# The even layer of a two-block network: four projection stages on tiles, rewritten as one stage of tile pairs with seven block products

## The reference, cut to what matters

```python
def even_layer(x, norm_g, w_in, pool_w, pool_scale, ws, bs, w_out):
    h = rmsnorm_2(x, norm_g)
    z = h @ w_in
    a, g_a, u, v, g_b = jnp.split(
        z, [A_WIDTH, 2 * A_WIDTH, 2 * A_WIDTH + B_WIDTH, 2 * A_WIDTH + 2 * B_WIDTH], axis=-1)
    y_a = multiscale_pool(a, pool_w, pool_scale) * jax.nn.silu(g_a)
    y_b = chunk_spatial_gate(u, v, ws, bs) * jax.nn.silu(g_b)
    return x + jnp.concatenate([y_a, y_b], axis=-1) @ w_out
```

## Time and profile before

| | us |
|---|---|
| median of 3 runs (3453.51 to 3455.23) | 3454.36 |
| the profiled execution, its own time | 3456.07 |
| its span in the profile | 3454.1 |
| PE busy | 3201.6 (93%) |
| DVE busy | 1726.1 (50%) |
| POOL busy | 1461.1 (42%) |
| ACT busy | 1195.2 (35%) |

### The profile page before, as it was taken

One profiled execution on the slowest core, in us unless ns is written; L12 is line 12 of the kernel. 1 busy time (PEld: TensorE's weight loads), 2 busy tenths in 40 slices (PEclk: granted clock), 3 DMA queues, 4 the chain that ended last, 5 costly groups with the idle time before them and its releaser, 6 DMA issues. The chain is left out here.

```text
span 3454.1 us, 43574 instructions
## 1 busy us (share of the span) xinstructions
PE 3201.6 (93%) x16242; PEld 2624.9 (76%) x16242; DVE 1726.1 (50%) x2541; ACT 1195.2 (35%) x2015; POOL 1461.1 (42%) x916
## 2 busy tenths in 40 slices
PE   4978997969599879999999799999999999999998
PEld 3767885857488757777887588888888888888877
DVE  4566224753799653311112565565555556555712
ACT  4256122732477621101101244443443444322311
POOL 2320331132422223333333265565565556688732
PEclk7989998989799999999999899999999999999999
DMA  8130113054699941141112211111111111222331
GB/s 288 43 86 30 41 40 102 2 178 140 243 397 396 335 135 45 31 146 52 43 43 97 72 49 46 47 56 44 55 45 48 47 46 56 66 75 74 112 104 68
DMA packets 310445, 347.46 MB, mean 101 GB/s; under 512 B 27894, under 2 KB 279722, under 8 KB 303986
## 3 DMA queue, kind: packets, MB, share of 16 engines
q1 hardware_dynamic: 299820, 308.21, 26.7%
q0 software_dynamic: 4608, 16.78, 1.9%
q10 hardware_dynamic: 5830, 19.98, 1.5%
HBM read 290.14 MB, written 51.38 MB: 99 GB/s over the span
## 5 line engine op out<-in xcount | busy, mean ns | idle before, releaser
L275 POOL TENSOR_TENSOR w_hi<-w_raw,zero_col 128x1024 fp32r<-128x1024 f32 x73 | 139.0, 1904 | 714.7 <-PE mls_z L310 205.3
L3087 POOL TENSOR_TENSOR odd_quarter_lo<-odd_w_sums,odd_quarter_hi 128x512 fp32r<-128x512 f32 x224 | 299.7, 1340 | 278.0 <-ACT odd_quarter_hi L3082 276.4
L3122 PE MATMUL first_z<-odd_t_hi,odd_quarter_hi 128*128 128x512 f32 x784 | 327.5, 418 | 18.7 <-DVE odd_t_lo L3830 18.7
L3122 PE MATMUL odd_z<-odd_t_hi,odd_quarter_hi 128*128 128x512 f32 x784 | 325.8, 416 | 0.1
L3124 PE MATMUL first_z<-odd_t_hi,odd_quarter_lo 128*128 128x512 f32 x784 | 308.4, 393 | 0.0
L3123 PE MATMUL first_z<-odd_t_lo,odd_quarter_hi 128*128 128x512 f32 x784 | 307.1, 392 | 0.0
L3124 PE MATMUL odd_z<-odd_t_hi,odd_quarter_lo 128*128 128x512 f32 x784 | 307.0, 392 | 0.0
L3123 PE MATMUL odd_z<-odd_t_lo,odd_quarter_hi 128*128 128x512 f32 x784 | 305.6, 390 | 0.0
L3087 POOL TENSOR_TENSOR odd_quarter_lo<-odd_raw,odd_quarter_hi 128x512 fp32r<-128x512 f32 x168 | 231.3, 1377 | 168.1 <-ACT odd_quarter_hi L3082 163.7
L3082 ACT CAST odd_quarter_hi<-odd_w_sums 128x512 fp32r<-128x512 f32 x224 | 139.6, 623 | 365.0 <-PE odd_z L3124 179.1
L3138 DVE SCALAR_TENSOR_TENSOR dil_set<-first_z,dil_set 128x512 f32<-128x512 f32 x196 | 170.6, 883 | 143.5 <-PE first_z L3124 138.4
(11 more groups left out here) (598 smaller groups left out, 7680.1 us busy)
## 6 DMA issues: line engine op xcount, KB each, us to landing
odd_raw<-in_odd_w_in SPq DMA_DIRECT2D x224, 256.0 KB, 3.1
raw_gate<-in_w_gate SPq DMA_DIRECT2D x16, 2048.0 KB, 16.2
raw_up<-in_w_up SPq DMA_DIRECT2D x16, 2048.0 KB, 15.1
raw_down<-in_w_down SPq DMA_DIRECT2D x16, 2048.0 KB, 15.7
w_raw<-in_even_w_in SPq DMA_DIRECT2D x40, 512.0 KB, 3.7
start_w_mod<-in_w_mod SPq DMA_DIRECT2D x11, 1024.0 KB, 10.9
w_raw<-in_w_in SPq DMA_DIRECT2D x16, 512.0 KB, 3.6
scan_w_mod<-in_w_mod SPq DMA_DIRECT2D x8, 1024.0 KB, 11.3
```

Of the source, the lines that this page charges most:

```text
L275: pool.tensor_tensor(w_hi[:, u], w_raw[:, u], zero_col[:, 0:1].to_broadcast([P, KT * P]).rearrange("p (k n) -> p k n", k=KT), ALU.add).the ...
L3087: pool.tensor_tensor(self.w_lo[:, n % self.SLOTS], self.source(m, i), self.w_hi[:, n % self.SLOTS].bitcast(F32), ALU.subtract).then_inc(se ...
L3122: pe.matmul(to, self.w_hi[:, slot, kt], t_hi[:, kt], start=(kt == 0), stop=False)
```

## The change

The even layer becomes one stage, `phase_even`, with the norm at its head. Its 40 projection tiles are taken in 20 pairs by `Quarters`: 8 pairs for the pool groups (per group one pair of `a` tiles and one pair of `g_a` tiles) and 4 triples of pairs (`v`, gate, `u`) for the spatial part. The mixing products (`mix_pool`, `turn_v`, `mix_spatial`) are put between block products of a later pair. The pool's running sums on DVE are cut in six parts (`pool_part`) that stand between the joins of the group's second pair. The `y` tiles are stored to DRAM and read back, and then one output product runs over all 2048 channels (`unit`: 16 units of 48 matmuls, one tile over half of the channels each), so the residual is read and written once. The prefetch in the expert stage is gone: the first weights are loaded at the head of the new stage. `Quarters` itself is unchanged but stands ahead in the file.

```diff
-        def phase_pool(next_parts, first_z):
...
-        def phase_spatial(next_parts, first_z):
...
-        def phase_even_norm(first_z):
...
+        phase_experts()
         first_z = ctx.enter_context(nc.psum_tensor("first_z", [P, 2, HALF], F32))
...
-        phase_even_norm(first_z)
-        phase_pool([even_a_out(u) for u in range(2)], first_z)
-        phase_out("even_a_out", y_hi, y_lo, even_a_out, 1, None, [even_cols(u, slice(SPATIAL_COLS[u], SPATIAL_COLS[u] + P)) for u in range(2)],
-                  first_z=first_z, first_done=True, next_rhs=(h_hi, h_lo))
-        phase_spatial([even_b_out(u) for u in range(2)], first_z)
...
+        def phase_even(first_z):
...
+            G, POOL_PAIRS, TRIPLES = len(POOL_SIZES), 2 * len(POOL_SIZES), KT // 2
+            PAIRS = POOL_PAIRS + 3 * TRIPLES
+            B11, T2_SUM, T3_SUM, T4_SUM, T1_SUM, B21, B22 = range(7)
...
+            quarters = Quarters("even", Arena(nc, quarters_at), PAIRS)
...
+            def pair_cols(m):
+                if m < POOL_PAIRS:
+                    return [pool_col(2 * m + t) for t in range(2)]
+                j, kind = (m - POOL_PAIRS) // 3, (m - POOL_PAIRS) % 3
+                return [SPATIAL_COLS[kind] + (2 * j + t) * P for t in range(2)]
...
+            def unit(k):
+                if k < 4:
+                    return k % 2, KT * (k // 2)
+                return k // 2, KT * (k % 2)
...
+                    for g in range(GROUPS):
+                        for j in (2 * g, 2 * g + 1):
+                            sp.dma_start(rows[:, j, :], ffn_rows[j * P:(j + 1) * P, :]).then_inc(rows_loaded[g], 16)
+                    load(0)
...
+                    for g in range(GROUPS):
+                        sp.wait_ge(added, KT * (g + 1))
+                        sp.dma_start(of_tokens(x_cm_k, g), of_tokens(even_xt, g)).then_inc(x_stored, 16)
+                    sp.wait_ge(x_stored, 16 * GROUPS)
+                    sp.wait_ge(scaled_done, GROUPS)
+                    load_matrices(0)
+                    load_matrices(1)
+                    for m in range(1, PAIRS):
...
+                    sp.wait_ge(y_done, KO)
+                    sp.dma_start(odd_x[:], x_cm_k).then_inc(x_loaded, 16)
+                    for k in range(4, 2 * KT):
+                        load_unit(k)
...
+                    for m in range(PAIRS):
+                        quarters.pool(pool, m)
...
+                    spread_out(3)
+                    pe.wait_ge(masked, 1)
+                    for g in range(G):
+                        ins = pe.transpose(aux[:, 1, g * CHUNK:(g + 1) * CHUNK], ws_low[:, g, :], ident)
+                    ins.then_inc(ws_turned, 1)
+                    def multiply(m, i, between=None):
+                        if m == 0:
+                            pe.wait_ge(t_lo_done, i + 1)
+                        quarters.multiply(pe, m, i, banks, even_tokens, between)
+                    def mix_pool(g, part):
+                        d, b = part // 2, part % 2
+                        if part == 0:
+                            pe.wait_ge(w_pool_loaded[g % 2], 16 * (g // 2 + 1))
+                            pe.wait_ge(pooled_done, 2 * g + 2)
+                            pe.wait_ge(y_done, 2 * g)
+                        for k in range(2):
+                            ins = pe.matmul((acc, aux)[d][:, b, :], w_pool[:, g % 2, k, d * P:(d + 1) * P], pooled[:, k, b * HALF:(b + 1) * HALF],
+                                            start=(k == 0), stop=(k == 1))
+                        if part == 3:
+                            ins.then_inc(pool_mixed, 1)
...
+                    for g in range(G):
+                        for i in range(7):
+                            multiply(2 * g, i)
+                            if g and 2 <= i < 6:
+                                mix_pool(g - 1, i - 2)
+                        for i in range(7):
+                            multiply(2 * g + 1, i)
+                    for j in range(TRIPLES):
+                        m = POOL_PAIRS + 3 * j
+                        for i in range(7):
+                            multiply(m, i)
+                            if j == 0 and 2 <= i < 6:
+                                mix_pool(G - 1, i - 2)
+                        for i in range(7):
+                            multiply(m + 1, i)
+                            if i < 2:
+                                turn_v(j, i)
+                        for i in range(7):
+                            multiply(m + 2, i)
+                            if 1 <= i < 5:
+                                mix_spatial(j, (i - 1) // 2, (i - 1) % 2)
+                    for k in range(2 * KT):
+                        n, first = unit(k)
+                        u = k % 2
+                        pe.wait_ge(wo_split, k + 1)
+                        if k < 2:
+                            pe.wait_ge(quarters.evicted, 7 * (PAIRS - 1) + (5, 7)[k])
+                        elif n >= 2 and first == 0:
+                            pe.wait_ge(z_free, n - 1)
+                        for kt in range(KT):
+                            c = first + kt
+                            if k in (0, 2):
+                                pe.wait_ge(y_lo_done, c + 1)
+                            for w, rhs, begin, end in ((wo_hi, y_hi[c], c == 0, False), (wo_hi, y_lo[c], False, False), (wo_lo, y_hi[c], False, c == KO - 1)):
+                                for b in range(2):
+                                    ins = pe.matmul(z[n % 2][:, b, :], w[:, u, kt], rhs[:, b * HALF:(b + 1) * HALF], start=begin, stop=end)
+                        ins.then_inc(projected, 1)
...
+                    square(3)
+                    root(2)
+                    quarters.hi(act, 0)
+                    quarters.hi(act, 1)
+                    root(3)
+                    act.wait_ge(scaled_done, 2)
+                    token_hi(B11, scaled[:, K1, T1])
+                    quarters.hi(act, 2)
+                    quarters.hi(act, 3)
+                    act.wait_ge(scaled_done, GROUPS)
+                    act.wait_ge(x_stored, 16 * GROUPS)
+                    token_hi(B21, scaled[:, K2, T1])
+                    token_hi(B22, scaled[:, K2, T2])
+                    for n, i in enumerate((T1_SUM, T2_SUM, T3_SUM, T4_SUM)):
+                        act.wait_ge(t_added, n + 1)
+                        token_hi(i, even_sums[i][:])
+                    def hi(m, i):
+                        quarters.hi(act, 7 * m + i + quarters.SLOTS)
...
+                        quarters.p1(act, m, banks, targets(m))
+                        hi(m, 0)
+                        if m < POOL_PAIRS + 1 and m % 2 == 0 and m:
+                            act.wait_ge(quarters.evicted, 7 * (m - 1) + 7)
+                            act.activation(silu[:], silu[:], ACT.Silu).then_inc(pool_silu, 1)
+                        if m >= POOL_PAIRS and kind == 2:
+                            act.wait_ge(quarters.evicted, 7 * (m - 1) + 7)
+                            act.activation(g_cm[:], g_cm[:], ACT.Silu).then_inc(spat_silu, 1)
+                        hi(m, 1)
+                        hi(m, 2)
...
+                    scale(3)
+                    b11, b12, b21, b22 = scaled[:, K1, T1], scaled[:, K1, T2], scaled[:, K2, T1], scaled[:, K2, T2]
+                    token_lo(B11, b11)
+                    dve.wait_ge(scaled_done, GROUPS)
+                    token_sum(T1_SUM, b12, b11)
+                    dve.wait_ge(t_added, 1)
+                    token_sum(T2_SUM, b22, even_sums[T1_SUM][:])
+                    token_sum(T3_SUM, b22, b12)
+                    dve.wait_ge(t_added, 2)
+                    token_sum(T4_SUM, b21, even_sums[T2_SUM][:])
+                    dve.wait_ge(t_added, 4)
+                    step = Steps(dve, dve_step)
+                    step(dve.memset(a_pad[0][:, :, 0:PAD], 0.0))
+                    step.wait()
+                    dve.sem_inc(pads_clear, 1)
+                    for i in (T2_SUM, T3_SUM, T4_SUM, T1_SUM):
+                        token_lo(i, even_sums[i][:])
...
+                            if k <= g:
+                                step(dve.tensor_tensor(sums[:, k % 2, PAD:], now[:, PAD:], now[:, PAD - (1 << k):PAD + SEQ - (1 << k)], ALU.add))
+                                continue
...
+                    def gate_spatial(j):
+                        dve.wait_ge(spat_silu, j + 1)
+                        dve.wait_ge(quarters.evicted, 7 * (POOL_PAIRS + 3 * j + 2) + 7)
+                        dve.wait_ge(y_stored, 16 * (G + j))
+                        dve.tensor_tensor(gated[:], u_cm[:], g_cm[:], ALU.mult).then_inc(gated_done, 1)
...
+                        m = 2 * g + 1
+                        pool_part(g, 0)
+                        u2(m)
+                        pool_part(g, 1)
+                        u3(m)
+                        pool_part(g, 2)
+                        c21(m)
+                        pool_part(g, 3)
+                        c22_u4(m)
```

(5 more changed lines are left out.)

959 lines of the change are left out of this document (510 added, 449 removed).

## The result

The changed kernel takes **3399.52 us** (median of 4 runs, 3396.94 to 3399.90) beside 3454.80 of the kernel before on the same chip: ratio 0.9835, 95% interval 0.9818 to 0.9853, so 1.65% less (the two medians alone divide to 0.9840). On another chip the same pair gave 0.9844 (0.9831 to 0.9857). The forecast of 3412 us is a ratio of 0.9877: the direction and the main term were right, the gain was put 12 to 14 us too small. The profiled execution took 3399.32 us with a span of 3397.2; it began the odd layer 53.5 us earlier than before (forecast: 42.8) and gained 3.4 us more behind it.

A forecast was written before the change was run, and what follows sets the result against it. The prediction took the even layer to be bound by PE's number of matmuls. Its terms summed to -42.8 us from 3456.07, giving 3413.3, and 3412 us as median; range of 8 in 10: 3399 to 3430, forecast's own 3402 to 3422.

The forecast's parts named there:

- block products: Even layer's projections on PE: 40 tiles of 48 matmuls become 20 pairs of 84, 19.04 us each; -54.4 us.
- stage switches: Even layer on PE: four switches between stages disappear with their waits; -20.7 us.
- later start: Head of the even layer: PE's first product waits for DVE's first token lo part, until 1256.3; +6.0 us.
- first pair: Even layer's first pair: PE waits for DVE's four sums and next lo, eight products taking 33.62 us; +11.9 us.
- insertions: Pool mixing in four pieces per group instead of one, each entry and exit costing 0.41 us; +4.9 us.
- turns of DVE and POOL: Pool groups' second pairs: two-SBUF-operand DVE instructions and POOL's exclude each other, POOL falls behind; +8 us, bounds 0 and 34.
- into the output product: Entry to the even layer's output product: a wait for weights queued behind the residual's load; +1.5 us.
- rival 2: Pool pairs: DVE and POOL turns cost nothing, POOL catches up in mixing time, start at early bound; 3400 us, chance 0.13.
- Rival 1: Pool pairs: DVE's sums and POOL's lo parts delay each other through all eight; +12 to +26, 3424 to 3438, chance 0.17.
- Rival 3: PE's clock slows after waits at every pool group, the sum loses 45 us; 3457 us, no change, chance 0.04.
- Rival 4: Even layer's pairs: joins take turns with POOL too, 23.4 us a pair instead of 19.04; 3492 us, slower, chance 0.03.
- Behind the output product: After the even layer's output product: same end of stage, odd layer's first matmuls wait on the same steps; 0 us.

The follow-up runs named there:

- experiment 2: Changed kernel with the fourth product of each even pair made twice, output unchanged: 3453.39 us, ratio 0.9992 to the kernel before.
- experiments 8 and 9: Changed kernel with DVE's and ACT's order ahead of both layers' first pair altered: 3401.17 us; the same plus three even-layer lo parts set to zero: 3398.04 us.
- Experiment 7: Changed kernel with each pool group's eight mixing matmuls in one piece instead of four pieces of two: 3400.95 us, ratio 0.9840 to the kernel before.
- experiment 5: Changed kernel in two variants: three slots instead of four for split weight quarters, 3412.56 us; three banks instead of four, 3410.09 us.
- experiment 6: Changed kernel with the pool mixing made over only the first half of each group's channels: 3389.43 us, ratio 0.9812 to the kernel before.
- experiment 4: Changed kernel with each of the 20 running sums of the pool groups made twice: 3418.40 us, ratio 0.9891 to the kernel before.

## Why the prediction was right and where it failed

The direction and the largest terms were right, and the time lies 0.5 us inside the range of 3399 to 3430, but by the ratio just outside it: 3399 us is 0.9840 of the kernel before, and 0.9835 was measured. Two terms were put too high, the turns of DVE and POOL and the insertions. In the order of its terms, forecast and then measured, for the even layer in the first pair of traces:

```
block products          -54.4    -54.4 (52.3 by experiment 2, plus the cover that it adds)
stage switches          -20.7    -20.7
later start              +6.0     +4.6
first pair              +11.9    +12.9
insertions               +4.9     +0.7
spatial extras            0       +0.8
turns of DVE and POOL    +8       +2.0
into the output product  +1.5     +0.4
sum                     -42.8    -53.7 (the odd layer's start: -53.5)
behind the odd start      0       -3.4
```

The switches are not measured apart: their 20.7 us are the remainder of the stretch before, which no longer exists, and the sum closes with them to 0.2 us, so an error of that remainder and one of another term could cancel. The spatial extras are 67.69 us for a triple (27.79, 20.86 and 19.04 between copies) less 3 x 19.04, over two channel tiles, 5.29 against 5.19. Into the output product: from pair 19's start, 2.85 us before its copy at 1696.33, to 1895.74 are 202.3 us, for 19.04 + 8.75 of mixing + 174.1.

- **Block products:** right. 84 matmuls take 19.04 us in the new stage as in the odd layer.
- **Start and first pair:** right in size. Eight products took 34.7 us (1254.93 to 0.2 us before the copy at 1289.83) against 33.6. But the step took DVE's chain alone for the cause; it is DVE's and POOL's turns (experiments 8 and 9).
- **Insertions:** the term was mis-sized, + 4.9 for + 0.7 (four groups of 7.06 us of mixing against 6.88). "The 0.41 us above" was the tile behind the mixing in the earlier trace rows, and I took all of it for a cost of each entry and exit. Experiment 7 gives 0.05 us for one.
- **The turns:** this step failed, + 8 for + 2.0. That the engines take turns by whole instructions was right: POOL's take 2.2 us for 1.29, and two of DVE's sums together 3.44 us (from 1429.25), 0.9 more than 2 x 1.26. Wrong was the sentence "POOL falls 7 us behind. Its lead at the start of a pair is 3.2 us", which sums the losses of a whole pair against a lead at its start. The lead is refilled to the slots' limit in the middle of each group's second pair, and POOL's 3.21 us waits for slots take up what was lost before. Only the second half's losses count, 2.3 us, and the lead there is 2.4. So the "some 4 us" of the last group came to 0.1 (19.13 for 19.04) and the 2 of the group of 8 tokens to 0.7 (19.76). The four small instructions, priced at 0.7 us in all, even took 3.68 in the last group, so the summed loss was larger than the prediction put it and still did not reach PE. With three slots instead of four the waits at these places do come to 8.0 us (experiment 5); that they meet the forecast's 8 is in part luck. DVE's own lag reaches PE once, 1.20 us with the wait of 1.00 at 1451.45, as the prediction said ("the mixing needs the pooled values 8.2 us into the next pair: one more").
- **Rivals:** rival 2 (it costs nothing, 3400 us, chance 0.13) was the closest, for the reason that it named in part: POOL catches up, but the catching up that counts is inside each pair and not in the mixing time (experiment 6). Rival 1 would need double the sums (experiment 4). Rival 3's slow clock appeared in the changed kernel only behind the first waits (granted clock 1.00 from 1290 us on); in variants it came back behind some waits of over 2 us (experiments 4, 5 and 8), so its mechanism is real and its condition was not met. Rival 4 is refuted by the pairs of 19.04 us with joins and POOL side by side.
- **"Behind the output product ... 0":** 1.6 of the 3.4 us are of the execution profiled before, the other 1.8 are of the last stores and were not foreseen. Their cause stays open.
- **The range** ended at 3399, because it took in rival 2; that the time came out at this edge owes as much to luck as to the sum. The forecast's own range, 3402 to 3422, missed: it was made of the near bounds of start, first pair and insertions and held the turns fixed at 8, though their near bound was 0 and they came out at 2.0.

## What to carry to other kernels

When two engines slow each other, do not sum the losses over a period: find the point in it where the slower engine waits for a free buffer, and sum only from there to the next instruction that is waited for. Try a cover by taking one buffer away: that made 8 us of waits visible which the finished kernel does not show. And before serving a first product sooner, count all work that must pass both engines ahead of the next group, since moving one product to the front only moves the wait.
